# Moving start-up work of a decoder kernel's first stage from VectorE and SyncE to GpSimd, and a sum of squares one tile on

## The reference

```python
ang = positions.astype(float32)[..., None] * inv_freq
q = partial_rope(rms_norm(q, q_norm_g), positions)
k = partial_rope(rms_norm(k, k_norm_g), positions)
```

## Time and profile before

| | |
|---|---|
| median of 3 runs | 1541.5 us (1540.37 to 1541.74) |
| the profiled execution | 1541.43 us, of which the traced span is 1539.7 us |
| PE busy | 1438.1 us (93%) |
| DVE, ACT, POOL busy | 895.0, 542.1, 385.7 us (58%, 35%, 25%) |
| mean granted clock of PE | 0.987 |

### The profile page before, as it was taken

One profiled execution on the slowest core, in us unless ns is written; L12 is line 12 of the kernel. 1 busy time (PEld: TensorE's weight loads), 2 busy tenths in 40 slices (PEclk: granted clock), 3 DMA queues, 4 the chain that ended last, 5 costly groups with the idle time before them and its releaser, 6 DMA issues.

```text
span 1539.7 us, 20207 instructions
## 1 busy us (share of the span) xinstructions
PE 1438.1 (93%) x7240; PEld 1211.1 (79%) x7240; DVE 895.0 (58%) x1524; ACT 542.1 (35%) x1270; POOL 385.7 (25%) x551
## 2 busy tenths in 40 slices
PE   2789999999889996789999999899999999999999
PEld 1677777788678786778888888688888888888887
DVE  7766667665444446887777775535456452645522
ACT  2433334433211116775666564322222222222200
POOL 2333333321222213454555555220000000000000
PEclk9999999999989998999999999999999999999999
DMA  8644555534987786756767765941111552112142
GB/s 315 226 144 168 196 196 192 193 118 169 336 313 293 259 310 220 254 213 257 262 251 277 271 242 196 328 130 41 55 42 62 171 191 76 42 55 74 50 150 82
DMA packets 96787, 285.62 MB, mean 186 GB/s; under 512 B 10768, under 2 KB 40496, under 8 KB 87088
## 3 DMA queue, kind: packets, MB, share of 16 engines
q1 hardware_dynamic: 87760, 250.74, 45.3%
q0 software_dynamic: 8928, 33.59, 6.3%
HBM read 196.22 MB, written 88.08 MB: 185 GB/s over the span
## 4 chain that ended last, share of the span: by engine, by line
PE 58%; DMA 4%; DVE 4%; ACT 3%; issue 2%; POOL 0%; ACTq 0%; SPq 0%; DVEq 0%; POOLq 0%
PE po_f_ps L1843 23%; PE po_y_ps L1859 11%; PE at_y_ps L1415 9%; PE ga_g_ps L933 5%; PE at_o_ps L1399 5%; PE at_s_ps L1371 3%; PE at_tr L1381 2%; DMA ga_ada<-in_ada_w 2%; ACT at_pr L1191 1%; DMA x_mid_t<-at_x 1%; DMA po_xn<-x_mid_t 1%; DVE at_sc L1265 1%; DMA silu_gates_t<-ga_sg 1%; DVE at_neg_max L1269 1%; DVE at_z L1289 0%
## 5 line engine op out<-in xcount | busy, mean ns | idle before, releaser
L1843 PE MATMUL po_f_ps<-po_ht,po_w 128*128 128x512 f32 x1536 | 348.9, 389 | 0.0
L1843 PEld LDWEIGHTS po_f_ps<-po_ht,po_w 128*128 128x128 f32 x1536 | 288.1, 188 | 60.1 <-DVE po_ht L1705 0.3
L667 PE MATMUL qk_proj<-qk_w_qkv,qk_ht 128*128 128x512 f32 x1152 | 282.6, 401 | 12.7 <-DVE qk_ht L460 6.7
L667 PEld LDWEIGHTS qk_proj<-qk_w_qkv,qk_ht 128*128 128x128 f32 x1152 | 217.1, 192 | 59.9 <-DVE qk_ht L460 8.0
L1415 PE MATMUL at_y_ps<-at_zt,at_w 128*128 128x512 f32 x768 | 198.6, 400 | 5.8 <-DVE at_x L1304 5.2
L1859 PE MATMUL po_y_ps<-po_zt,po_w 128*128 128x512 f32 x768 | 174.7, 389 | 0.0
L1859 PEld LDWEIGHTS po_y_ps<-po_zt,po_w 128*128 128x128 f32 x768 | 144.1, 188 | 29.9
L1415 PEld LDWEIGHTS at_y_ps<-at_zt,at_w 128*128 128x128 f32 x768 | 138.4, 190 | 31.6 <-issue 7.1
L1692 DVE TENSOR_TENSOR po_w<-po_raw,po_w 128x1024 fp32r<-128x1024 f32 x48 | 58.8, 1225 | 129.1 <-ACT po_w L1626 129.1
L1147 POOL TENSOR_SCALAR_AFFINE_SELECT at_pt<-at_ph 128x512 fp32r<-128x512 f32 x128 | 83.6, 677 | 187.2 <-ACT at_ph L1198 187.2
L306 POOL TENSOR_TENSOR qk_rq<-qk_mq,qk_half 128x8 f32<-128x8 f32 (+1 forms) x48 | 70.2, 1462 | 189.4 <-DVE qk_mq L487 189.4
(11 more groups left out here) (168 smaller groups left out, 1985.8 us busy)
## 6 DMA issues: line engine op xcount, KB each, us to landing
at_w<-out_weight_split SPq DMA_DIRECT2D x32, 1024.0 KB, 6.6
queries_t<-qk_late SPq DMA_DIRECT2D x16, 1024.0 KB, 4.3
ga_ada<-in_ada_w POOLq DMA_DIRECT2D x64, 256.0 KB, 4.6
at_qt<-queries_t SPq DMA_DIRECT2D x16, 1024.0 KB, 8.2
ht_split<-qk_ht SPq DMA_DIRECT2D x6, 2048.0 KB, 9.6
values_split<-qk_late SPq DMA_DIRECT2D x16, 768.0 KB, 5.0
at_vs<-values_split SPq DMA_DIRECT2D x16, 768.0 KB, 5.0
qk_late<-in_ada_w SPq DMA_DIRECT2D x16, 512.0 KB, 5.6
```

What stands on the lines that cost most here:

```text
L667: last = nc.tensor.matmul(proj[:, b * BANK:(b + 1) * BANK], ht[:, s % 2, m, k, t * P:(t + 1) * P], w_qkv[:, w, k, b * BANK:(b + 1) * BANK] ...
L1843: last = nc.tensor.matmul(f_ps[:, bank(j, h), :], w[:, i % 2, a, k, :], ht[:, h, m, k, :], start=(n == 0), stop=(n == 3 * KC - 1))
```

## The change

- The four small loads go from SP's queue, between x and the sixth piece of ada_w, to POOL's queue, ahead of `add_squares(0)`.
- `reduce_angle` goes from DVE to POOL, behind `rstd_x(0)`. [...] The scratch tile `back` lies in `rot_a`.
- ACT computes sine and cosine behind `w_high(7)`, directly ahead of the first bank's square, and that square no longer waits for `pre_done` 9 but for the cosine (`act_begun` 3). The four small DVE instructions (`set_gains`) go behind `normalise(0, 1)`, ahead of q's gains and rotation.
- ACT does `w_high(8)` to `w_high(10)` after the first square, `w_high(11)` after the second, then squares chunks 0 to 4 of block 1, and chunks 5 to 7 after the third bank's square. POOL adds them after the second bank's power, all seven ahead of the third bank's power.
- PE sums block 1's columns after `project(1, 0)`; DVE's `mean_x(1)` comes after `mean_squares(1, 0)`, POOL's `rstd_x(1)` ahead of `rstd(1, 0)`, and PE's `spread(1)` behind the transposes of q rounds 0 and 1, ahead of `project(1, 1)`.
- In the attend stage the 16 folds count their high and low splits of both operands on one semaphore each instead of two. The order of the work stays, and each wait stands for the same event (PE has one wait less per fold).

```diff
@@ sync
             if i == AS - 1:
                 load_x(0)
-                sp.dma_start(bias[:, :], ada_b[0]).then_inc(small_loaded, 16)
-                sp.dma_start(g_col[:, :], norm_g[0]).then_inc(small_loaded, 16)
-                sp.dma_start(gq[:, :], q_norm[0].partition_broadcast(P)).then_inc(small_loaded, 16)
-                sp.dma_start(gk[:, :], k_norm[0].partition_broadcast(P)).then_inc(small_loaded, 16)
@@ gpsimd
+        def reduce_angle(part, quarter, dst):
+            done = [10 * part]
+
+            def then(ins):
+                done[0] += 1
+                ins.then_inc(trig_step, 1)
+                pool.wait_ge(trig_step, done[0])
+
+            then(nc.gpsimd.tensor_scalar(turns, ang, 1.0 / TWO_PI, quarter, ALU.mult, ALU.add))
+            then(nc.gpsimd.tensor_scalar(turns, turns, MAGIC, None, ALU.add))
+            then(nc.gpsimd.tensor_scalar(turns, turns, MAGIC, None, ALU.subtract))
+            for n, part_of_turn in enumerate((C1, C2, C3)):
+                then(nc.gpsimd.tensor_scalar(back, turns, -part_of_turn, None, ALU.mult))
+                then(nc.gpsimd.tensor_tensor(dst, back, ang if n == 0 else dst, ALU.add))
+            then(nc.gpsimd.tensor_scalar(dst, dst, quarter * TWO_PI, None, ALU.add))
+            nc.gpsimd.tensor_scalar(dst, dst, LIMIT, -LIMIT, ALU.min, ALU.max).then_inc(trig_arg, 1)
...
+        pool.dma_start(bias[:, :], ada_b[0]).then_inc(small_loaded, 16)
+        pool.dma_start(g_col[:, :], norm_g[0]).then_inc(small_loaded, 16)
+        pool.dma_start(gq[:, :], q_norm[0].partition_broadcast(P)).then_inc(small_loaded, 16)
+        pool.dma_start(gk[:, :], k_norm[0].partition_broadcast(P)).then_inc(small_loaded, 16)
         add_squares(0, range(KC))
         rstd_x(0)
+        pool.wait_ge(vec, HALF + 1)
+        reduce_angle(0, 0.0, red)
+        reduce_angle(1, 0.25, red2)
         pool.wait_ge(mod_summed, len(MOD_PARTS))
         nc.gpsimd.memset(vs, 0.0).then_inc(consts_set, 1)
         for n in range(NB):
             if n > 0 and n % 2 == 0 and n // 2 + 1 < NS:
                 rstd_x(n // 2 + 1)
             for b in range(BANKS):
+                if n == 1 and b == 0:
+                    rstd_x(1)
                 rstd(n, b)
-                if n == 0 and b == 0:
+                if n == 0 and b == 1:
                     add_squares(1, range(KC))
-                if n == 0 and b == 1:
-                    rstd_x(1)
                 add_squares(*squared(n, b))
@@ scalar
         square_x(0, range(KC))
-        act.wait_ge(trig_arg, 1)
-        nc.scalar.activation(sin[:, :, HALF:ROT], red, ACT.Sin).then_inc(act_begun, 1)
-        act.wait_ge(trig_arg, 2)
-        nc.scalar.activation(cos[:, :, 0:HALF], red2, ACT.Sin).then_inc(act_begun, 1)
...
         for i in range(RAW + 1, RAW + AS):
             w_high(i)
-        act.wait_ge(pre_done, 9)
+        act.wait_ge(trig_arg, 1)
+        nc.scalar.activation(sin[:, :, HALF:ROT], red, ACT.Sin).then_inc(act_begun, 1)
+        act.wait_ge(trig_arg, 2)
+        nc.scalar.activation(cos[:, :, 0:HALF], red2, ACT.Sin).then_inc(act_begun, 1)
         for n in range(NB + 1):
             front = n < NB
             if front:
+                if n == 0:
+                    act.wait_ge(act_begun, 3)
                 square(n, 0)
                 if n == 0:
-                    w_high(8)
-                    w_high(9)
-                    square_x(1, range(KC))
+                    for i in range(8, 11):
+                        w_high(i)
...
                 square(n, 1)
-                for i in range(10, ITEMS) if n == 0 else ():
-                    w_high(i)
+                if n == 0:
+                    w_high(11)
+                    square_x(1, range(SQ + 1))
...
                 square(n, 2)
+                if n == 0:
+                    square_x(1, range(SQ + 1, KC))
@@ vector
         for i in range(ADA):
             add_ada(i)
-            if i == 4:
-                reduce_angle(0.0, red)
-            if i == 9:
-                reduce_angle(0.25, red2)
             if i == ADA - 7:
                 mean_x(0)
...
-        dve.wait_ge(act_begun, 3)
...
-        dve.wait_ge(pre_done, 9)
...
             if front:
                 mean_squares(n, 0)
+            if n == 1:
+                mean_x(1)
...
             if front:
+                if n == 0:
+                    set_gains()
                 gains_and_rotation(n, 0)
                 low_q(n)
-                if n == 0:
-                    mean_x(1)
                 modulate(*modulated(n, 2))
@@ tensor
             project(pe, n, 0)
             if n == 1:
-                spread(pe, 1)
+                sum_squares(pe, 1)
...
             if n > 0:
                 q_round(pe, n - 1, 0)
                 q_round(pe, n - 1, 1)
+            if n == 1:
+                spread(pe, 1)
             project(pe, n, 1)
...
             project(pe, n, 2)
-            if n == 0:
-                sum_squares(pe, 1)
@@ attend_stage, fold
             if h == 0:
-                pe.wait_ge(wg_lo, f + 1)
-                pe.wait_ge(fold_lo, u + 1)
+                pe.wait_ge(fold_lo, wv_split(u))
                 wait(pe, fold_out, u - 1)
```

More of the change, by code:

```diff
@@ L173, in qkv_stage @@
     ang, turns, red, red2 = (trig[:, i] for i in range(4))
+    back = rot_a[:, 0:HALF, :].rearrange("p a r -> p (a r)").rearrange("p (n r) -> p n r", r=HALF)
     ps = psum_layout(nc, "qk_", [("proj", [P, QKV]), ("tr", [P, 3, BANK]), ("st_ps", [P, BANK]), ("bc_ps", [P, BANK])])
@@ L184, in qkv_stage @@
     trig_arg, pre_done = sem("trig_arg"), sem("pre_done")
+    trig_step = sem("trig_step")
     ada_added, mod_summed = sem("ada_added"), sem("mod_summed")
@@ L550, in set_scale, with set_gains @@
             dve.wait_ge(pre_done, 2 * part + 1)
[L552 to L560, removed]
+        def set_gains():
+            dve.wait_ge(act_begun, 3)
+            nc.vector.tensor_copy(cos[:, :, HALF:ROT], cos[:, :, 0:HALF]).then_inc(pre_done, 1)
+            nc.vector.tensor_scalar(sin[:, :, 0:HALF], sin[:, :, HALF:ROT], -1.0, None, ALU.mult).then_inc(pre_done, 1)
+            nc.vector.tensor_scalar(gq[:, :], gq[:, :], float(HD) ** -0.5, None, ALU.mult).then_inc(pre_done, 1)
+            dve.wait_ge(pre_done, 8)
+            nc.vector.tensor_tensor(gk[:, ROT:HD], gk[:, ROT:HD], gq[:, ROT:HD], ALU.mult).then_inc(pre_done, 1)
+            dve.wait_ge(pre_done, 9)
         dve.wait_ge(act_begun, 1)
@@ L1017, in attend_stage, with wg_split, wv_split @@
     fold_loaded, wg_loaded, fold_stored = ring("fold_loaded", 3), ring("wg_loaded", 2), ring("fold_stored", 2)
-    fold_hi, fold_lo, wg_hi, wg_lo, fold_done, fold_out = (sem(n) for n in (
-        "fold_hi", "fold_lo", "wg_hi", "wg_lo", "fold_done", "fold_out"))
+    fold_hi, fold_lo, fold_done, fold_out = (sem(n) for n in ("fold_hi", "fold_lo", "fold_done", "fold_out"))
+    def wg_split(f):
+        return f * (PAIRS + 1) + 1
+    def wv_split(u):
+        return wg_split(u // PAIRS) + u % PAIRS + 1
     LAST = UNITS + BEHIND
@@ L1064, in load_fold @@
         if pair == 0:
-            wait(sp, wg_lo, f - 1)
+            if f >= 2:
+                sp.wait_ge(fold_lo, wg_split(f - 2))
             sp.dma_start(wg_raw[:, f % 2], w_group[GC * f:GC * (f + 1)].rearrange("c p n -> p c n")).then_inc(wg_loaded[f % 2], 16)
-        wait(sp, fold_lo, u - 2)
+        if u >= 3:
+            sp.wait_ge(fold_lo, wv_split(u - 3))
         sp.dma_start(wv_raw[:, u % 3], wvt[GC * f:GC * (f + 1)][:, :, pair * ROWS:(pair + 1) * ROWS].rearrange("c p n -> p c n")).then_inc(fold_loaded[u % 3], 16)
@@ L1223, in fold_high @@
                 wait(act, fold_done, PAIRS * (f - 1))
-                nc.scalar.activation(wg[:, f % 2, HI], wg_raw[:, f % 2], ACT.Copy).then_inc(wg_hi, 1)
+                nc.scalar.activation(wg[:, f % 2, HI], wg_raw[:, f % 2], ACT.Copy).then_inc(fold_hi, 1)
             act.wait_ge(fold_loaded[u % 3], 16 * (u // 3 + 1))
@@ L1309, in fold_low @@
             if u % PAIRS == 0:
-                dve.wait_ge(wg_hi, f + 1)
-                nc.vector.tensor_tensor(wg[:, f % 2, LO], wg_raw[:, f % 2], wg[:, f % 2, HI].bitcast(F32), ALU.subtract).then_inc(wg_lo, 1)
-            dve.wait_ge(fold_hi, u + 1)
+                dve.wait_ge(fold_hi, wg_split(f))
+                nc.vector.tensor_tensor(wg[:, f % 2, LO], wg_raw[:, f % 2], wg[:, f % 2, HI].bitcast(F32), ALU.subtract).then_inc(fold_lo, 1)
+            dve.wait_ge(fold_hi, wv_split(u))
             nc.vector.tensor_tensor(wv[:, u % 3, LO], wv_raw[:, u % 3], wv[:, u % 3, HI].bitcast(F32),
```

## The result

The changed kernel takes 1545.96 us (median of 8 runs, 1544.42 to 1548.63), the one before 1540.85 us (8 runs beside them, 1538.51 to 1542.31). The ratio is 1.0032 with a 95% interval of [1.0022, 1.0041], about 5 us: a small loss, but beyond the 0.2% that the prediction took for no change. The forecast was 1543.1 with a range up to 1545.6: the sign was right, the size is outside the range. The profiled execution took 1545.82 us, span 1544.1, against 1541.43 and 1539.7: 4.4 us more.

What follows compares the result with a forecast made beforehand. TensorE, busy 93% of the span, bounds the kernel, so the start of `project(2, 0)` is the measure. Against the profiled 1541.4 us, +0.5 and +1.1 make 1543.0, or 1543.1 by the median; range 1538.9 to 1545.6.

Steps and rivals of the forecast that it cites:

- Head, lead 2.7: Start-up to `mean_x(0)`: without the small loads ahead, the sixth piece lands at about 14.95, `mean_x(0)` at 25.0; ends 0 and 3.3.
- Rival C: Start-up: the small loads still delay, sharing the same DMA engines; head's lead 1 us or less, 1544.8 us; chance 0.1.
- Range work on POOL: Behind `rstd_x(0)`: 22 chained POOL instructions, 10.3 us in the clear, done near 49.7 (ends 45 and 54); DVE's loss 0.
- rival B: Ahead of tile 0: POOL's range work costs DVE up to 2.7 us or comes late; 1544 to 1546 us; chance 0.22.
- Sines: Behind `w_high(7)` on ACT: table load 1.28, two sines 0.31 each; first square at 51.8 instead of 54.98, lead 3.2.
- To `w_low(11)`: First square to `normalise(0, 1)`: lengths kept, load issued at 57.0, `normalise(0, 1)` at 64.9 instead of 68.36, lead 3.4.
- Tile 0's tail: `normalise(0, 1)` to `normalise(0, 2)`: gains and POOL's additions delay bank 2's power; `normalise(0, 2)` at 74.6, lead down to 0.4.
- The new wait: Ahead of `project(1, 1)`: TensorE waits of 0.9 and 2.4 us; start at 77.6 instead of 76.93, lag 0.7.
- Clock: At `project(1, 1)`: a clock drop after the second new wait costs some 1.7 us; two thirds, 1.1, taken.
- The rest at nothing: `w_high(8)` to `(10)` earlier, block 1's squares later, and the folds' counters in the attend stage: 0.

Runs made afterwards that it cites:

- a_late_gains: The changed kernel with the two broadcast gain loads moved to SyncE behind the load of weight piece 10; 1543.85 us, ratio to the kernel before 1.0019.
- b_strided_loads: The kernel before with both gain loads late and two same-size loads of separate rows in their place; one execution, 1541.24 us beside 1541.31.

## Why the prediction was wrong, by its steps

1. *Head, lead 2.7: this step failed.* It should have been -0.4, and the sixth piece came at 18.15, which the prediction itself had named as a sign of being wrong. I priced the loads' own transfer at nothing and took the queue's order for the cause of the late sixth piece; the cause was the two broadcast loads, which stall the transfers beside them for 3 us on either queue. With both broadcasts out of the way the rest of the step was exact (25.17 for a forecast 25.0). Rival C named this and had 0.1; "they share the same DMA engines" was in my own text, with at most 1 us. The earlier trace rows had the evidence: the sixth piece came 4.34 us behind x where 1.25 were due, and the 80 KB of the four small loads don't fill 3 us at 418 GB/s. Of this error of 3.1 us only 1.5 arrive at `project(2, 0)`: that much sooner it starts with the head put right (a_late_gains).
2. *Range work on POOL: right in its end, but its price for DVE was put at nothing.* Its 22 instructions (11 each time, as each of DVE's three fused steps is two on POOL) took 30.18 to 49.98: eight of them 1.07 to 1.54 us, beside DVE's additions and low parts, the others 0.30 to 0.88. The forecast end of 49.7 assumed an earlier start; in the event POOL was faster during `modulate`. ACT did not wait for it. DVE did lose: its first three `w_low` took 4.10 us instead of 3.66, `w_low(3)` 1.48 instead of 1.23, and the first `hx` came 0.86 us later than before, of which 0.44 is `mean_x(0)`'s lag. From `mean_x(0)` to `w_high(4)` it took 21.73 us instead of 20.91, in a_late_gains too. So rival B's price was real but small, some 0.8 us where the forecast had 0.
3. *Sines: right.* Table load 1.28, sine 1.30 after its start (forecast 1.3), first square right behind the cosine. The Trainium skill (ScalarE: Activation LUTs, "What ACT_TABLE_LOAD costs") adds a drain of some 1.4 us; both load rows here, before and after, show none. From `w_high(7)` (ends 53.77) to the square it was 1.85 us, forecast 2.0.
4. *To `w_low(11)`: better than said by about 1.5 us*: -0.64 at the square became +1.05 at `normalise(0, 1)`, because the last load landed 4.3 us after its issue, not 5.6 (not explained), and POOL's power was no longer in the way.
5. *Tile 0's tail: right in kind, too small.* From `normalise(0, 1)` to `split_q` I had 1.3 us more, it was 2.0 (4.50 against 2.50): the gain and the first rotation step took 0.85 and 0.84 instead of 0.42, `set_gains` 1.25 instead of 0.74. POOL's last addition ended 2 us after ACT's last square of block 1 (74.33), and bank 2's power started behind it at 76.42: exactly the mechanism forecast. Lead lost from step 4 to `normalise(0, 2)`: 3.5 us, forecast 3.0.
6. *The new wait: right in sum, not in place.* Lag at `project(1, 1)` grew by 1.2 us (2.44 to 3.63), forecast 1.1. TensorE waited 1.89 us for the additions (forecast 0.9) and, after the sum and the transposes, 0.4 more for `rx` (forecast 2.4). The second wait was short as sum and transposes ran at the half clock, 0.97 and 1.95 us instead of 0.50 and 1.04; in a_late_gains, where they took 0.61 and 1.07, the waits were 2.24 and 1.64.
7. *Clock: it fell, and already behind the first wait.* From 76.5 to 83.4 us the granted clock is 0.51; `project(1, 1)` took 7.07 instead of 5.72, 1.35 us (forecast 1.1, as two thirds of 1.7), and spread and transposes were slower too. `project(2, 0)` gave back 1.03 (7.61 instead of 8.64), by where its slow stretch happened to end.
8. *The rest at nothing: nothing in the traces against it.*

a_late_gains shows what the other steps were worth, as its head is the forecast one. Its points against the forecast are: first square 52.64 (51.8), `normalise(0, 1)` 64.74 (64.9), `normalise(0, 2)` 75.25 (74.6), `project(1, 1)` 78.34 (77.6), `project(2, 0)` 98.32 (96.9 with the clock). So DVE's 0.8 us of step 2 is there at the first square and made good by step 4. At `project(1, 1)` the tail is 0.7 us behind the forecast, and from there to `project(2, 0)` another 0.7 is lost: with the clock at half for the first part of it (0.50 from 77.4 to 80.5 us) `project(1, 1)` took 7.75 us, 2.0 more than at full clock, where the forecast had put down 1.1. Of the miss of 2.9 us at `project(2, 0)` (99.85 for 96.9) 1.5 thus go to step 1 and 1.4 to steps 5 to 7. The forecast's steps pass an error of the head on whole; that only half of it arrived is luck. Between these two kernels 3.0 us lie at the first square, 2.6 at `normalise(0, 1)`, 2.2 at `project(1, 1)` and 1.5 at `project(2, 0)`, the last step by where the clock stood at half (7.75 us for `project(1, 1)` against 7.07).

## What to carry to other kernels

In this kernel two loads that each broadcast one short row over all partitions stalled the transfers beside them for 3 us, on either queue, and their bytes did not tell. Such a load is one to try late, outside a busy start. When a transfer arrives late, compare its distance to the one ahead with its bytes over the bandwidth before blaming the queue's order. A lead gained at the start is worth what the next order of waits lets through: here a reduction whose result the next matmul group needed stood one step ahead of that group on a chain of four engines, and its old place, one tile earlier, was worth 3 us.

## What the runs showed of the hardware

- Two broadcasts of 256 bytes to 128 partitions held back all other loads for about 3 us, from SyncE's queue and from GpSimd's (98 GB/s from 8 to 11 us with loads queued; on SyncE's queue 61 GB/s from 13 to 15 us), while two loads of 128 separate rows of 256 bytes cost 0.3 us. Why reading one row is slow was not tried, nor whether one such load alone does it.
- A GpSimd instruction of 128x128 with one input took 0.30 us at the shortest and 1.31 beside DVE additions with two inputs in SBUF. The Trainium skill (SBUF — State Buffer, "SBUF: two separate sides") calls this an exclusive lock; for POOL the traces agree. DVE's additions lost 0.18 us each beside POOL's 256-column additions here (4.66 for three against 1.37 each alone), not the whole 0.72.
- GpSimd's DMA issues took 0.53 to 0.68 us each and cost nothing there.
- A lead changes on its way to the end: b_strided_loads was 1.6 us ahead at `project(2, 0)`, 3.1 late in the gate stage (column sums at 523.21 against 526.33) and 0.2 at the end. What changed it was not traced. Under 3 us the start of `project(2, 0)` was the better measure of a step, the interval over five rounds the judge of the whole.
